# A fused layer kernel on one core: the order of the work in front of the first expert slots, and a first mixer tile that runs three slots later

## The reference, cut to what matters

```python
h = modulate(rms_norm(x, g_norm1), shift1, scale1)
proj = h @ w_in                       # a | u | v
mixed = concat([pool_mixer(a), spatial_gating(u, layer_norm(v))])
x = x + gate1 * (mixed @ w_out)
h = modulate(rms_norm(x, g_norm2), shift2, scale2)
q = h @ w_query                       # 8 heads x 2 sides x 128
scores = q . sub_keys                 # 128 keys for each of the 16 sides
s_top, i_top = top_k(scores, 16)      # for each side
best, sel = top_k(s_top[0][:, None] + s_top[1][None, :], 16)
idx = expert ids of sel;  gate = softmax(best)
act = gelu(expert_down[idx] . h)      # 16 experts x 8 heads for each token
x = x + gate2 * sum(gate * act * expert_up[idx])
out = rms_norm(x, g_final)
```

## Time and profile before

| | us |
|---|---|
| median of three runs (2825.89 to 2829.47) | 2828.95 |
| the profiled execution, its own time | 2833.91 |
| its span in the profile | 2832.1 |

### The profile page before, as it was taken

How to read it: one execution, slowest core, us unless ns; L and a number is a source line. 1 busy time by engine, 2 the same in 40 slices (tenths; PEclk the granted TensorE clock), 3 DMA queues, 4 the chain that set the end, 5 groups by cost and what they waited for, 6 DMA issues and landing times.

```text
span 2832.1 us, 38640 instructions
## 1 busy us (share of the span) xinstructions
PE 1938.6 (68%) x13316; PEld 893.8 (32%) x13316; DVE 1894.8 (67%) x4714; ACT 1210.7 (43%) x3867; POOL 1123.1 (40%) x1030
## 2 busy tenths in 40 slices
PE   5898898888886566666656666665666666665553
PEld 4555354444442222232323222221322323221110
DVE  5686776785766567677666757677676756676454
ACT  1245445454453344454444434444343544344333
POOL 0044334344443254444444444444444444344342
PEclk9998898899886566665666667665766666576555
DMA  9899999999999999999999999999999999999997
GB/s 404 339 373 403 396 413 417 409 420 420 420 401 397 416 422 421 421 421 421 421 421 421 421 421 419 416 421 421 417 415 421 419 421 416 421 415 421 421 420 294
DMA packets 169221, 1162.38 MB, mean 410 GB/s; under 512 B 19009, under 2 KB 25665, under 8 KB 35778
## 3 DMA queue, kind: packets, MB, share of 16 engines
q0 software_dynamic: 147456, 1073.81, 91.9%
q1 hardware_dynamic: 21570, 86.11, 7.7%
HBM read 1151.97 MB, written 7.86 MB: 410 GB/s over the span
## 4 chain that ended last, share of the span: by engine, by line
DMA 54%; PE 22%; DVE 11%; ACT 6%; issue 3%; SPq 3%; POOL 0%; another core or an unknown queue 0%; DVEq 0%; POOLq 0%; ACTq 0%
DMA work<-experts,expert_rows 41%; DMA more_ring<-experts,expert_rows 8%; PE ps_sum L900 7%; DVE work L1560 5%; PE ps_small L866 5%; PE ps_m L815 4%; DMA work<-w_ada 2%; PE ps_m L759 2%; DMA weights<-experts,expert_rows 1%; ACT diag L1137 1%; ACT weight L1132 1%; DMA vn_u<-x_scratch 1%; PE ps_wide L841 1%; SPq L613 1%; PE ps_m L770 1%
## 5 line engine op out<-in xcount | busy, mean ns | idle before, releaser
L650 POOL DMA_INDIRECT work<-experts,expert_rows x818 | 899.0, 1099 | 1378.7 <-PE ps_sum L900 1225.8
L1560 DVE CUSTOM_DVE_ANT_0 work<-work 128x1024 f32<-128x1024 f32 x818 | 997.5, 1221 | 589.3 <-DMA work<-experts,expert_rows 573.4
L900 PE MATMUL ps_sum<-work,diag 128*32 128x256 f32 x6544 | 717.5, 523 | 674.7 <-ACT diag L1137 653.6
L1130 ACT ACTIVATE act_out<-act_in 128x1 f32<-128x1 f32 x1024 | 207.4, 203 | 1162.8 <-DVE act_in L1560 1141.9
L900 PEld LDWEIGHTS ps_sum<-work,diag 128*32 128x32 f32 x6544 | 150.1, 126 | 1146.5 <-ACT diag L1137 1052.1
L1137 ACT ACTIVATE diag<-const,weight 128x32 f32<-128x32 f32 x1024 | 329.2, 321 | 33.5
L1132 ACT ACTIVATE weight<-gate,act_out 128x1 f32<-128x1 f32 x1024 | 301.6, 295 | 33.3
L866 PE MATMUL ps_small<-h_t,weights 128*128 128x128 f32 x1344 | 291.2, 384 | 0.0
L866 PEld LDWEIGHTS ps_small<-h_t,weights 128*128 128x128 f32 x1344 | 249.3, 278 | 125.7 <-issue 120.4
L1560 DVE CUSTOM_DVE_ANT_0 more_ring<-more_ring,work 128x1024 f32<-128x1024 f32 x122 | 149.1, 1222 | 91.5 <-DMA more_ring<-experts,expert_rows 90.4
L650 POOL DMA_INDIRECT more_ring<-experts,expert_rows x122 | 134.8, 1105 | 180.3 <-PE ps_sum L900 175.5
(11 more groups left out here) (200 smaller groups left out, 1991.1 us busy)
## 6 DMA issues: line engine op xcount, KB each, us to landing
work<-w_ada SPq DMA_DIRECT2D x12, 2048.0 KB, 23.6
work<-sides SPq DMA_DIRECT2D x26, 576.0 KB, 8.4
work<-experts,expert_rows POOLq DMA_INDIRECT x818
weights<-sides SPq DMA_DIRECT2D x16, 576.0 KB
more_sides<-sides SPq DMA_DIRECT2D x12, 576.0 KB
weights<-w_in SPq DMA_DIRECT2D x3, 2048.0 KB, 17.2
x_buf<-x SPq DMA_DIRECT2D x8, 512.0 KB, 11.4
weights<-w_out SPq DMA_DIRECT2D x2, 2048.0 KB, 37.5
```

The source lines that it names most:

```text
L650: nc.gpsimd.indirect_dma_start(ring[x.ring], None, experts, bass.IndirectOffsetOnAxis(ap=rows_flat[:, x.column:x.column + 1], axis=0),).th ...
L900: last = nc.tensor.matmul(ps_sum[quarter(c), x.group, :], diag[:, x.ring, :], ring[x.ring][:, D + c * QCOLS:D + (c + 1) * QCOLS], start=x. ...
L1130: nc.scalar.activation(act_out[:, s:s + 1], act_in[:, s:s + 1], ACT.Gelu).then_inc(s_gelu, 1)
L1560: nc.vector.tensor_tensor_reduce(down, down, h2_spread[x.segment % 2], 1.0, 0.0, ALU.mult, ALU.add, act_in[:, x.g % TURN:x.g % TURN + 1]). ...
```

## The change

Four things move; no instruction's work is altered, and each engine computes the same.

1. `MIX_AT[1]` goes from -9 to -6 and `MIX_HEAD` from 9 to 6: three steps of tile 1's mixer that stood in front of slot 0 go into the slots, and every later one stands three slots later (`RESIDUAL` in slot 28 instead of 25). Tiles 2, 3 and 4 go two slots later.
2. The fourth side of turn 1 leaves the stretch in front of slot 0: `SIDE_AT[0] = (1, 3)` puts its query in slots 0 and 1, its copy in 2, its scores in 3 and the copy of the scores in 4. SP's list loads one side fewer in front, and that one from the slots.
3. Turn 1's routing starts in slot 5 instead of 2. By the plan of the bank, 5 + 19 = 24 does not fit before the copies in 25 to 28, so its `move_choices` stands in slot 29 instead of 21 and its `place_choices` on DVE in slot 30 instead of 22.
4. In front of slot 0, PE scores the first side of turn 1 between the two halves of the spread of h2 and moves routing 1's choices before the mixer's projection; ACT takes routing 1's exp before the copies of the mixer.

```diff
-MIX_HEAD = PROJECT_A
-MIX_AT = {1: -MIX_HEAD, 2: 31, 3: 70, 4: 109, 5: 150, 6: 190, 7: 230}
+MIX_HEAD = PROJECT_V + 1
+MIX_AT = {1: -MIX_HEAD, 2: 33, 3: 72, 4: 111, 5: 150, 6: 190, 7: 230}
...
-ROUTE_AT = [None, 2, 28, 50, 74, 98]
+ROUTE_AT = [None, 5, 28, 50, 74, 98]
...
+SIDE_AT[0] = (1, 3)
...
-            for n in range(2, 6 + SIDE_BUFS):
+            for n in range(2, 5 + SIDE_BUFS):
                 load_side(*FIRST_USE[n])
...
             move_choices(0)
-            for half in range(2):
-                spread_first_h2(0, half)
+            spread_first_h2(0, 0)
+            side(1, 0)
+            spread_first_h2(0, 1)
             mixer(TURN_H, 1)
-            for b in range(2):
-                side(1, b)
-                scores(1, b)
+            scores(1, 0)
+            side(1, 1)
+            move_choices(1)
+            scores(1, 1)
             for n in range(TURN_H + 1, MIX_HEAD):
                 mixer(n, 1)
-                if n == PROJECT_V + 1:
-                    move_choices(1)
-            for b in range(2, 4):
-                side(1, b)
-                scores(1, b)
+            side(1, 2)
+            scores(1, 2)
...
             exp_logits(0)
-            for half in range(2):
-                copy_spread(0, half)
-            for n in range(SCALE_H + 1, MIX_HEAD):
-                mixer(n, 1)
-            for b in range(4):
-                if b == 2:
-                    exp_logits(1)
-                copy_query(1, b)
-                copy_score(1, b)
+            copy_spread(0, 0)
+            copy_query(1, 0)
+            copy_spread(0, 1)
+            exp_logits(1)
+            copy_score(1, 0)
+            mixer(COPY_H, 1)
+            copy_query(1, 1)
+            mixer(COPY_H + 1, 1)
+            copy_score(1, 1)
+            copy_query(1, 2)
+            copy_score(1, 2)
```

## The result

| | median of the plain runs | lowest to highest | runs |
|---|---|---|---|
| before | 2826.27 us | 2823.19 to 2832.24 | 20 |
| changed | 2831.68 us | 2828.78 to 2834.18 | 20 |

The ratio on record is 1.0015, with an interval of 1.0009 to 1.0022, or 4.2 us; the medians lie 5.4 us apart. The time is inside the range and near the middle of the case that had most of the chance; 2831 us was forecast. The number is nearer than its working deserves: the median of before that it started from was 2828.95 us, and with 20 runs it is 2826.27 us. I said plus 2 us; measured are plus 5.4, and 4.8 when the changed kernel was run again (e1).

A forecast was written before the change was run, and what follows sets the result against it. It took DMA gathers to bound the kernel, so only idle queue time counts: 2833.91 + 1.4 (parts 1 to 5) + 0.5 (part 6) = 2835.8 for a profiled execution, 5.0 above the median, hence 2831 us; range 2823 to 2838.

The forecast's parts named there:

- the case that had most of the chance: Whole kernel: the forecast itself, 2831 us, with a range of its own of 2827 to 2834.5; chance 0.48.
- Part 1: Ahead of slot 0, routing 1's choices: exp and move come earlier, gather 4 at 123.8 instead of 129.38, 5.6 us sooner.
- Part 2: Slot 0: PE loses 8.9 us of work ahead of the first add; gather 7 at 133 instead of 142.
- Part 3: Slots 0 to 6: returned steps make DVE wait 8.5 us at NORM_V, 3 for the fourth side; slot 18 within 1 us.
- Part 4: Tile 1's output projections, slots 19 to 26: start about 187.5, take 26 us, end at 213.9, 6.7 us later.
- Part 5: Gather of slot 32: issued at 221.7 into an empty queue, dot 6.0 us later; parts 1 to 5 net 1.4 us late.
- Part 6: Tiles 2 to 4 two slots later: same steps, about 2 us either way, 0.5 us of loss taken.
- a rival on tile 1's projections: Low clock after waits in slots 13 to 18: first three projection steps 1.9 us dearer each, 2836.5 us; chance 0.20.
- The shift is the larger effect: Tiles 2 to 4: output burst crosses a turn's move, up to 4 us either way, 2827 or 2835 us; chance 0.07.
- The order of the first head's lists does nothing: Ahead of slot 0: parts 1 and 2 shrink to some 3 us, part 5's loss stands alone, 2833 us; chance 0.08.
- The early gain survives: Up to slot 32: projections end by 208.5, gather 32 meets a non-empty queue, 5 us stay, 2824 us; chance 0.17.
- signs of being wrong: Gather 32 issued before 217, slot 32's dot under 223 or over 232, or a new DMA hole behind slot 64.

The follow-up runs named there:

- e3: Changed kernel with the mixers of tiles 2 to 4 back in the slots of before (31, 70, 109): 2828.19 us, ratio 0.9999 to before.
- e12: Changed kernel with five idle filler multiplies on PE, three in slot 55 and two in slot 57: 2827.78 us, ratio 1.0001 to before.
- e6: Kernel before with only the mixers of tiles 2 to 4 moved two slots later: 2831.07 us, ratio 1.0012 to before.
- e10: Changed kernel with turn 1's choices placed in slot 25 instead of 30, route steps unmoved: 2832.93 us, ratio 1.0010 to before.
- e4: Changed kernel with turn 1's routing one slot sooner, choices placed in slot 24, and tiles 2 to 4 back: 2835.78 us, ratio 1.0023 to before.
- e2: Changed kernel with turn 1's routing from slot 4 instead of 5, choices placed in slot 24: 2831.70 us, ratio 1.0014 to before.
- e11: Changed kernel with choices placed in slot 25 and ten filler multiplies on PE in slots 55 to 57: 2829.91 us, ratio 1.0007 to before.

## Why the prediction was right or wrong

- **Part 1, right.** Counted from gather 0's issue, gather 4 comes after 9.9 us; 12.8 were forecast (123.8 less 110.97), 18.4 stood in the profile. Part of that gain belongs to the profiled execution of before: against the second one it is 5.3 us, near the 5.6 forecast. DVE's wait for ACT's exp, 6.76 us in the first, was 3.54 in the second.
- **Part 2, right in kind.** Gather 7 comes 17.7 us behind gather 0 (22.0 forecast, 31.0 and 27.8 before), 10.1 us sooner than in the second execution; 9 were forecast.
- **Part 3, right in kind, the wait for `NORM_V` nearly twice too long.** DVE waits for `NORM_V` and for the fourth side, 4.46 and 2.12 us (8.5 and 3 forecast), since the last step to v ends at 133.5 us and not at 140.1. Its dot of slot 18 stands 0.9 us ahead of the second execution's, within the 1 us that was forecast, and 4.2 us ahead of the first's. The lead at slot 31 is 7.4 us in the profile after.
- **Part 4, too long.** Tile 1's output projections start in slot 19 at 183.62 us and end at 207.7; 187.5 and 213.9 were forecast. The list takes 24.1 us and not 26. Of the sooner start 2.0 us are gather 0, issued at 108.99 and not 110.97 us.
- **Part 5, the mechanism as forecast.** `RESIDUAL` waits for PE, the choices are placed behind slot 30's dot, POOL idles 11.59 us, the queue runs empty. Gather 32 is issued 7.0 us sooner than forecast, its dot stands 6.6 us behind the issue (6.0 taken). Its row has landed 1.0 us later than in the second execution of before, its dot starts 0.8 us sooner; forecast was a dot 1.4 us late. Parts 1 to 5 cost 0.6 us by e3 and −0.2 by e12 (which gives the shift's cost back too), nothing that can be measured.
- **Part 6 is the step that failed.** "The same steps, and both PE and DMA move together", bounded by "about 2 us either way", 0.5 us taken: it measured 4.1 us (e6). I bounded it by DMA's idle time in the profile of before and not by what PE's clock would be at the place to which the burst moves. I had seen the mechanism, and put it as a rival on tile 1's projections, at slots 13 to 18: the low clock came there (0.50 in 176 to 182 us), but the projections were entered at full clock (0.97 in 182 to 188, a first step of 1.88 us). It struck tile 2's, in the same kernel, by the same cause, a run of waits for DVE ahead of the burst.
- **The rivals.** "The shift is the larger effect" had 0.07 and 2835 us; it is what happened, with the mechanism of the one that had 0.20. "The order of the first head's lists does nothing" fell with gather 4. "The early gain survives" was wrong, and would have been wrong without the gate too (e10).
- **The signs.** Three of the signs of being wrong came. Gather 32 was issued at 214.65 us, before 217, and slot 32's dot started at 221.26, under 223; 2.0 us of both are gather 0's sooner issue, most of the rest is what part 4 had too long. And there is a new hole in DMA at 305 to 320 us, where the gathers of slots 65 to 69 are issued, which is part 6. Gathers 4 and 7 came at 118.86 and 126.69 us and not near 124 and 133, and DVE stood 4.46 us at `NORM_V` and not 7 to 9.

That the total came out close is luck. The median of three runs from which it started was 2.7 us high and parts 1 to 5 were priced some 0.8 to 1.6 us too dear; the shift was priced 3.6 us too low. These nearly cancel.

## What to carry to other kernels

Before a burst of matmuls on the critical path is moved, look at what PE does in the few microseconds ahead of its new place: if it waits there for a busy engine, the burst may start at half clock, as here, and all that hangs on it is late by the difference. Filling those waits, and no more than those, with idle multiplies gave the time back. A hole in DMA's share is worth closing only if what frees the buffers behind it can keep the lead. Here it could not (e10), and closing the hole put the load of the next tile behind a full queue. And a kernel's profiled execution should be set against its median, and if it can be against a second one, before anything is read off it: 2.4 of the 6.0 idle us that looked like the kernel's were gone in the second execution.

## What the runs showed of the hardware

- The same program may get a low or a full clock in the same stretch: 0.54 and 0.50 in one execution, 0.92 and 0.79 in the other (106 to 118 us). The next gathers lie 3.2 us apart, of which about half is the clock and the rest a wait of ACT whose releaser the profile does not know.
- PE's waits of 2.64, 0.37 and 2.02 us in three slots led to a clock of 0.50 in 300 to 305 us; with fillers that left gaps of 0.98 and 1.04 us it stayed at 1.00.
- A 512 KB load on SP's queue took 6.1 to 6.4 us from issue to landing where the gathers' queue had run empty ahead of slot 32, 11.8 to 12.6 us in before and e6, and 12.5 to 16.9 us in e4, e2, e11 and e10, where the gathers' queue was kept full.
- A gather of 1 MB into an empty queue had its dot 6.6 us behind its issue (214.65 to 221.26 us). The Trainium skill, "DMA: Bandwidth & Descriptors", section "Anatomy of one DMA — SWDGE (gpsimd) path", gives about 2.0 us beside the bytes, an estimate of 4.4 us; the trace is 2.2 us over it, with the store and load of x and the gathers issued right behind it sharing the engines.
